# Gate blocks turned by the vector engine, and softplus at the seam of slots 0 and 1

## The reference

```
proj = h @ w_in                       # q, k, v, g, xb, gate, 1024 columns each
xc   = conv_b + sum_t xp[:, t:t+S] * conv_w[t]           # causal, 4 taps, on xb
r, i = sigmoid(xc @ w_a + b_a), sigmoid(xc @ w_x + b_x)  # by blocks of 128
log_a = -8 * r * softplus(-lam);  a = exp(log_a)
h_t  = a_t * h_{t-1} + sqrt(1 - a_t^2) * i_t * xc_t
lru  = h * gelu(gate)                 # tanh form
y    = concat(retention, lru) @ w_out
```

## Time and profile before

| | |
|---|---|
| median of 3 runs | 2010.25 us (2009.47 to 2010.56) |
| the profiled execution's own time | 2009.5 us |
| its span | 2007.7 us |
| TensorE (PE) busy | 1996.0 us, 99% |
| VectorE (DVE) busy | 1450.2 us, 72% |
| ScalarE (ACT) busy | 1026.2 us, 51% |
| GpSimd (POOL) busy | 45.2 us, 2% |
| granted TensorE clock | 0.999 |

### The profile page before, as it was taken

The page is one execution under the profiler, slowest core; times in us unless marked ns, Lnnn a source line. Parts: engine busy times, 40 slices in busy tenths (PEclk is TensorE's granted clock), DMA queues, the critical chain, the costliest instruction groups (busy, mean ns, idle before and its releaser), DMA issues.

```text
span 2007.7 us, 24673 instructions
## 1 busy us (share of the span) xinstructions
PE 1996.0 (99%) x9155; PEld 1651.2 (82%) x9155; DVE 1450.2 (72%) x2023; ACT 1026.2 (51%) x1354; POOL 45.2 (2%) x55
## 2 busy tenths in 40 slices
PE   9999999999999999999999999999999999999998
PEld 7888888888888888888888877888888888888886
DVE  6777778987558647846888887988548756854875
ACT  6665665455345435444545665555435434534554
POOL 1110110000000000000000000000000000000000
PEclk9999999999999999999999999999999999999999
DMA  8556546566556556565656544565565555566563
GB/s 304 186 170 215 172 164 210 189 192 207 189 188 202 195 188 189 197 198 174 204 189 194 174 157 156 182 205 192 193 197 193 191 191 187 186 209 189 188 205 109
DMA packets 191437, 382.48 MB, mean 191 GB/s; under 512 B 6265, under 2 KB 7041, under 8 KB 191233
## 3 DMA queue, kind: packets, MB, share of 16 engines
q1 hardware_dynamic: 190112, 377.58, 57.2%
q0 software_dynamic: 1216, 3.88, 0.6%
q10 hardware_dynamic: 32, 0.01, 0.0%
HBM read 379.34 MB, written 2.10 MB: 190 GB/s over the span
## 4 chain that ended last, share of the span: by engine, by line
PE 96%; DVE 3%; ACT 1%; issue 0%; DMA 0%; SPq 0%; ACTq 0%; DVEq 0%
PE acc L1151 31%; PE acc L1153 31%; PE acc L1152 31%; DVE area L1007 2%; DVE w_lo L817 1%; PE bank L1182 1%; PE bank L1259 0%; ACT area L703 0%; DMA x<-in_x 0%; PE bank L1269 0%; ACT w_hi L600 0%; PE acc L1172 0%; PE acc L1171 0%; PE acc L1173 0%; DVE b_lo L978 0%
## 5 line engine op out<-in xcount | busy, mean ns | idle before, releaser
L817 DVE TENSOR_TENSOR w_lo<-raw,w_hi 128x1024 fp32r<-128x1024 f32 x712 | 864.4, 1224 | 502.1 <-ACT w_hi L600 499.2
L600 ACT ACTIVATE w_hi<-raw 128x1024 fp32r<-128x1024 f32 x712 | 747.6, 1060 | 771.8 <-PE acc L1153 768.5
L1151 PE MATMUL acc<-w_hi,a_hi 128*128 128x512 f32 x1568 | 613.7, 391 | 0.0
L1153 PE MATMUL acc<-w_hi,a_lo 128*128 128x512 f32 x1568 | 610.3, 389 | 0.0
L1152 PE MATMUL acc<-w_lo,a_hi 128*128 128x512 f32 x1568 | 610.1, 389 | 0.0
L1151 PE MATMUL acc<-w_hi,b_hi 128*128 128x512 f32 x1264 | 492.3, 389 | 0.0
L1152 PE MATMUL acc<-w_lo,b_hi 128*128 128x512 f32 x1264 | 491.7, 389 | 0.0
L1153 PE MATMUL acc<-w_hi,b_lo 128*128 128x512 f32 x1264 | 491.7, 389 | 0.0
L1151 PEld LDWEIGHTS acc<-w_hi,a_hi 128*128 128x128 f32 x1568 | 294.4, 188 | 61.9 <-issue 1.5
L1153 PEld LDWEIGHTS acc<-w_hi,a_lo 128*128 128x128 f32 x1568 | 294.3, 188 | 61.4
L1152 PEld LDWEIGHTS acc<-w_lo,a_hi 128*128 128x128 f32 x1568 | 294.4, 188 | 60.4
(11 more groups left out here) (172 smaller groups left out, 561.0 us busy)
## 6 DMA issues: line engine op xcount, KB each, us to landing
raw<-in_mlp_w_up SPq DMA_DIRECT2D x128, 1024.0 KB, 5.3
raw<-in_mlp_w_down SPq DMA_DIRECT2D x128, 1024.0 KB, 5.1
raw<-in_hyb_w_in SPq DMA_DIRECT2D x44, 1024.0 KB, 5.3
raw<-in_attn_w_qkv SPq DMA_DIRECT2D x20, 1024.0 KB, 5.1
raw<-in_hyb_w_out SPq DMA_DIRECT2D x16, 1024.0 KB, 5.2
raw<-in_attn_w_out SPq DMA_DIRECT2D x16, 1024.0 KB, 5.1
raw<-in_hyb_w_in SPq DMA_DIRECT2D x8, 512.0 KB, 9.3
out_y<-x SPq DMA_DIRECT2D x4, 512.0 KB, 3.0
```

Of the source, the lines that this page charges most:

```text
L600: nc.scalar.activation(w_hi[:, h % RING], raw[:, h // 2, 2 * (h % 2):2 * (h % 2) + 2, :], ACT.Copy).then_inc(hi_ready, 1)
L817: nc.vector.tensor_tensor(w_lo[:, h % RING], raw[:, h // 2, 2 * (h % 2):2 * (h % 2) + 2, :], w_hi[:, h % RING].bitcast(F32), ALU.subtract) ...
L1151: nc.tensor.matmul(a, xh, wh, start=first, stop=False)
L1153: ins = nc.tensor.matmul(a, xl, wh, start=False, stop=last)
```

## The change

Gate joins the kinds that VectorE turns (`DIRECT`): sixteen transposes of 32 x 256 from `stage` into `gate_t`, six in tick 0 and ten in tick 2 of slots 2 and 8. TensorE's eight transposes and VectorE's two copies of each gate block go. The convolution of groups 0 and 4, which lies in the same two slots, moves from tick 2 to tick 1, between the six and the ten. Softplus is split: its first two instructions move to tick 6 of slot 0, ScalarE's exponential to tick 7 of slot 0, ahead of the first root, and the fifteen others to tick 0 of slot 1, behind the first `inverse`.

```diff
-DIRECT = {"xb", "kv", "aq"}
+DIRECT = {"xb", "gate", "kv", "aq"}
...
-FROM_STAGE = {"gate"}
-
-TURN_AT = {"q": 4, "k": 4, "g": 4, "gate": 2}
+FROM_STAGE = set()
+
+TURN_AT = {"q": 4, "k": 4, "g": 4}
...
+QUADRANTS_AT["gate"] = {0: 6, 2: 10}
...
-CONV_AT = [2, 1, 1, 2]
+CONV_AT = [1, 1, 1, 2]
...
                 if k == 7:
+                    act.wait_ge(vecs_ready, 2)
+                    act.wait_ge(soft_abs, 1)
+                    nc.scalar.activation(soft[:, 1, :], soft[:, 0, :], ACT.Exp, scale=-1.0).then_inc(soft_exp, 1)
                     root(0)
...
-                    if slot.i is None and b == 1 and k == 6:
-                        act.wait_ge(vecs_ready, 2)
-                        act.wait_ge(soft_abs, 1)
-                        nc.scalar.activation(soft[:, 1, :], soft[:, 0, :], ACT.Exp, scale=-1.0).then_inc(soft_exp, 1)
...
+            def softplus_abs():
+
+                lam = vecs[:, V_LAM:V_LAM + LRU_BLOCKS]
+                link(nc.vector.tensor_scalar(soft[:, 2, :], lam, -1.0, None, ALU.mult))
+                nc.vector.tensor_tensor(soft[:, 0, :], lam, soft[:, 2, :], ALU.max).then_inc(soft_abs, 1)
+
             def softplus():
...
-                link(nc.vector.tensor_scalar(nl, lam, -1.0, None, ALU.mult))
-                nc.vector.tensor_tensor(ab, lam, nl, ALU.max).then_inc(soft_abs, 1)
                 dve.wait_ge(soft_exp, 1)
...
-                    tile = {"xb": xb_t[:, :, TAPS - 1:], "kv": kk_t, "aq": qq_t}[kind]
+                    tile = {"xb": xb_t[:, :, TAPS - 1:], "gate": gate_t, "kv": kk_t, "aq": qq_t}[kind]
...
-                tile = {"gate": gate_t, "q": q_t, "k": k_t}[kind]
+                tile = {"q": q_t, "k": k_t}[kind]
...
+                if k == 6:
+                    dve.wait_ge(zeroed, 1)
+                    dve.wait_ge(table_loaded, 1)
+                    dve.wait_ge(vecs_ready, 2)
+                    softplus_abs()
                 if k == 7:
                     mean_square(0, TT * COLS)
...
-                    if slot.i is None and b == 1 and k == 6:
-                        dve.wait_ge(zeroed, 1)
-                        dve.wait_ge(vecs_ready, 2)
+                    if slot.i is None and b == 1 and k == 0:
                         softplus()
```

More of the change, by code:

```diff
@@ L867, in rotate @@
                 nc.vector.tensor_tensor(y2, y2, tmp[:, 1], ALU.add).then_inc(rotated, 1)
+            def softplus_abs():
+                lam = vecs[:, V_LAM:V_LAM + LRU_BLOCKS]
+                link(nc.vector.tensor_scalar(soft[:, 2, :], lam, -1.0, None, ALU.mult))
+                nc.vector.tensor_tensor(soft[:, 0, :], lam, soft[:, 2, :], ALU.max).then_inc(soft_abs, 1)
             def softplus():
-                lam = vecs[:, V_LAM:V_LAM + LRU_BLOCKS]
                 ab, z, nl, s, s2, p, neg8, pos4 = (soft[:, i, :] for i in range(8))
-                link(nc.vector.tensor_scalar(nl, lam, -1.0, None, ALU.mult))
-                nc.vector.tensor_tensor(ab, lam, nl, ALU.max).then_inc(soft_abs, 1)
                 dve.wait_ge(soft_exp, 1)
```

## The result

The changed kernel takes 2012.85 us (median of 20 runs, 2012.21 to 2014.09) against 2010.13 of the kernel before (20 runs): ratio 1.0013, 95% interval 1.0007 to 1.0019. It is 2.7 us slower, which many runs can tell although it lies under the 0.2% that the prediction set for a difference. The forecast was +0.8 and 2011.1, with a range up to 2012.4: the time is above the range, by 0.45 us.

A forecast was written before the change was run, and what follows sets the result against it. The prediction took TensorE, issuing without a gap in the first 300 us, as the bound. It summed -1.74 (transposes) + 0.34 (softplus) + 2.24 (port turns) to +0.8 us, a median of 2011.1 us, range 2008.3 to 2012.4.

The forecast's parts named there:

- The transposes leave TensorE: Slots 2 and 8: eight transposes per gate block leave TensorE's chain, 0.87 us each time, gain 1.74 us.
- Softplus at the seam: Slots 0 to 1: moved softplus delays VectorE 0.63 us, stalling the last half of slot 1 by 0.34 us.
- The exponential without its own table load: ScalarE, slot 0: exponential ahead of the root needs no load, cost 0; rival with a load 2012.3 us, chance 0.07.
- The turns at the port: GpSimd's gate polynomial alternates with VectorE's `w_lo`s, 4.7 us instead of 2.77; half 5 of slots 3 and 9 stalls 1.13.
- a port that costs little: Rival: polynomial ends within 3.4 us, ScalarE under 0.47 late, only the seam is paid; -1.4, 2008.9 us, chance 0.33.
- elsewhere near the change it is 2 to 7 us: Slack between a `w_lo`'s end and its first product, apart from thin places in slots 1, 3 and 9.
- Sum of the mixer: First 300 us: -1.74 + 0.34 + 2.24 = +0.8 us.
- Two things only can move the time there: First 300 us: only work taken out of TensorE's queue, or a half whose weights come late, changes the time.
- a late load of weights: Rival: `raw` is freed too late and a missed SyncE turn costs a load, 5.3 us; 2016.4 us, chance 0.02.
- The range: Whole kernel: 2008.3 to 2012.4 us, from below the cheap-port rival to the table-load rival; forecast's own range 2010.2 to 2011.9.

The follow-up runs named there:

- e4: Kernel before without any turning of gate: TensorE's transposes left out, VectorE's two copies read `stage` unturned; 2010.70 us, ratio 1.0003.
- e8: Changed kernel in which the three `w_lo` behind the ten transposes read PSUM in place of `raw`, one SBUF operand instead of two; 2011.03 us, ratio 1.0004.
- e5: Changed kernel with the gate's ten transposes in tick 1, ahead of the convolution, instead of tick 2; 2012.36 us, ratio 1.0011.
- e1: Changed kernel with 40 extra waits on a long-reached semaphore in TensorE's program ahead of the first MLP loop; 2010.96 us, ratio 1.0004.
- e9: Kernel before, work unchanged, with 221 extra instructions (waits on long-reached semaphores) in TensorE's program in slots 1 to 15; 2012.17 us, ratio 1.0011.
- e10: Changed kernel with ten transposes in tick 1, groups 0 and 4's convolution in the slot before, softplus in two parts, no extra waits; 2010.64 us, ratio 1.0004.
- e11: Changed kernel with 36 extra waits in TensorE's program behind the first MLP loop (slots 42 to 46); 2013.10 us, ratio 1.0016.
- e12: Changed kernel with 20 extra waits on a long-reached semaphore in TensorE's program ahead of the first MLP loop; 2020.38 us, ratio 1.0050.

## Why the prediction was wrong, step by step

- *The transposes leave TensorE, -1.74.* Right: the half in which they stood is 0.82 and 0.80 shorter in slots 2 and 8, and the slower restart behind them (0.11) goes too, -1.85; e4, which changes nothing else in TensorE's program, gives -1.73 over slots 0 to 11.
- *Softplus at the seam, +0.34.* Measured 0.34. The mechanism is right; that the number is right to 0.01 is luck: the `w_lo` comes 0.49 later instead of 0.63 and the product follows it by 0.06 instead of 0.12, which is less, and the restart of 0.10 was not in the sum, which is more.
- *The exponential without its own table load, 0.* Right: ScalarE goes from it at 33.63 straight to the root's load at 33.84, and the root is on time. ScalarE has one instruction less (1353 for 1354), the load of the old place.
- *The turns at the port.* Right: polynomial 4.66 for 4.7, stalls 1.11 and 1.09 for 1.13. Slots 3 and 9 as wholes last 1.0 us longer, 0.2 less in all than the two stalls. e8 and e5 show the cause, and that the rival, a port that costs little, fails. Two readings were off without harm: the gate comes 1.8 us later against its slot in slot 8, but 1.1 in slot 2, whose polynomial starts at 69.75 instead of 68.40; and "elsewhere near the change it is 2 to 7 us" overlooks half 2 of slot 2, which has 0.17 us of slack behind softplus in the kernel before. Since softplus leaves that slot, nothing came of it.
- *Sum of the mixer, +0.8.* Measured +0.51.
- *The sum, which ends at 300 us.* This is the step that failed. "Two things only can move the time there" is true of the first 300 us; the sum -1.74 + 0.34 + 2.24 then has no term for the 1700 behind them, which it takes as moved in one piece, at nothing and without a reason. They are moved so, but for the heads of the loop, where TensorE's instructions have to be there. The loop is not touched by the change; its place in the program is. The missing term measures +2.1 us, and e1, e4, e9, e10 and e11 put and remove it. The rivals had a late load of weights, nothing of late instructions, though the profile of before has the row: its page says `q8 instruction: 48`, and by stretches those reads pause during the loop's later passes. Such a pause can be lost.
- *The range* was made of the terms' own bounds. With the loop's place unknown it would have had to reach 2 us further up, and by e12 some 9.

The time lies within 0.2% of the kernel before, as forecast, but with this many runs it is a loss beyond its interval.

## What to carry to other kernels

When a program's length changes ahead of a loop, the reads of the instruction queue per pass are part of the comparison: count them in both profiles (48 or 66 here) before explaining a difference by work. A change of 2 us in 2000 can be the loop's place alone, and some waits that wait for nothing can move it back (e1: -1.9). Try more than one number of them: half of them made it 7.5 us worse (e12). And when an engine is given more work, follow it to the engines that wait for its results: here GpSimd got its data 1.1 and 1.8 us later and, what was worse, just as three VectorE instructions stood in line with which it takes turns (4.7 us instead of 2.8).

## What the hardware showed that I had not expected

- A loop of 1614 instructions of TensorE (103 KB, 6.3 reads of 16 KB) can be kept from pass to pass or read again in each one (18 reads more). The first MLP loop is kept where it begins at place 69 or 70 of its block and read again at 34, 35 and 52. But the second MLP loop, of the same length, is kept in every kernel, at 57 (before), 23 (after), 22 (e9) and 40 (e12). So the place of the first instruction in its block is not the whole rule, as 40 lies between 35 and 52. What else decides stays open; shown is that the reads and the stalls of the first loop come and go with where it begins, moved by waits that do no work. The counts are of the programs as built, and may be off by a few.
- TensorE's granted clock went from 1.00 to 0.57 behind a gap of 2.9 us (products 0.43 us apart instead of 0.23, for 3.4 us); a gap of 0.85 did not do that, nor the longest of the others at these heads, 1.46 us in e9.
- Waits on reached semaphores cost TensorE next to nothing here: with 221 of them in slots 1 to 15, slots 0 to 11 take 288.76 us instead of 288.71.
